# A two-layer decoder trunk on one core: norm inputs scaled ahead on GpSimd, squares added there, waits tile by tile, and an output projection in K halves

## The reference

```python
for l in range(DEPTH):                       # 2 layers
    mod = (c_act @ p['w_ada'][l] + p['b_ada'][l])[:, None, :]
    sh1, sc1, g1, sh2, sc2, g2 = split_cols(mod, [D_MODEL] * 6)
    h = rms_norm(x, p['norm_mix'][l]) * (1.0 + sc1) + sh1
    y = even_mixer(h, ...) if l % 2 == 0 else odd_mixer(h, ...)   # in-projection, recurrence and
                                             # pooling / convolution, out-projection @ w_out
    x = x + g1 * y
    h = rms_norm(x, p['norm_mlp'][l]) * (1.0 + sc2) + sh2
    x = x + g2 * sq_relu_mlp(h, p['mlp_w_up'][l], p['mlp_w_down'][l])
y = rms_norm(x, p['norm_final'])
```

## Time and profile before

| what | value |
|---|---|
| median of three runs | 2791.52 us (2789.2 to 2792.09) |
| the profiled execution | 2792.04 us, of it span 2789.5 us |
| TensorE matmul busy | 2628.9 us (94%), mean granted clock 0.967 |
| VectorE busy | 1583.7 us (57%) |
| ScalarE busy | 985.7 us (35%) |
| GpSimd busy | 276.3 us (10%) |
| chain that ended last | TensorE 82%, VectorE 8%, DMA 6% |
| DMA | 616.13 MB, mean 221 GB/s |

### The profile page before, as it was taken

The page is one execution under the profiler, slowest core; times in us unless marked ns, Lnnn a source line. Parts: engine busy times, 40 slices in busy tenths (PEclk is TensorE's granted clock), DMA queues, the critical chain, the costliest instruction groups (busy, mean ns, idle before and its releaser), DMA issues.

```text
span 2789.5 us, 54649 instructions
## 1 busy us (share of the span) xinstructions
PE 2628.9 (94%) x22440; PEld 2457.6 (88%) x22440; DVE 1583.7 (57%) x2332; ACT 985.7 (35%) x1079; POOL 276.3 (10%) x250
## 2 busy tenths in 40 slices
PE   6799989989999999999997999988899999999998
PEld 3389878979999999999996998988899999999998
DVE  2346354465445545545545998984565565565653
ACT  1133324333223322332333444444343333333333
POOL 1102050010000000000002334530100000000000
PEclk9599999999999999999998999998999999999999
DMA  9977887869999999999753454453455555555553
GB/s 327 336 247 227 281 249 250 276 216 299 301 300 297 297 297 297 297 298 297 236 166 120 151 159 155 136 178 100 144 168 181 181 181 181 181 181 183 181 176 106
DMA packets 589978, 616.13 MB, mean 221 GB/s; under 512 B 10431, under 2 KB 584093, under 8 KB 589313
## 3 DMA queue, kind: packets, MB, share of 16 engines
q1 hardware_dynamic: 583154, 591.70, 67.4%
q0 software_dynamic: 6720, 22.96, 2.6%
HBM read 602.77 MB, written 13.26 MB: 221 GB/s over the span
## 4 chain that ended last, share of the span: by engine, by line
PE 82%; DVE 8%; DMA 6%; issue 1%; ACT 1%; POOL 1%; SPq 0%; DVEq 0%; ACTq 0%; POOLq 0%
PE ps L743 24%; PE ps L744 23%; PE ps L745 23%; PE pm L806 5%; DMA araw_first<-in_w_ada 3%; DVE h_lo L1774 2%; DMA out_new_gla_sample<-st 1%; DVE z L2073 1%; PE pm L821 1%; PE pm L908 1%; DVE w_lo L1650 1%; DMA out_new_hgrn_sample<-st 1%; PE pm L759 1%; DVE acc L2073 1%; PE ps L806 1%
## 5 line engine op out<-in xcount | busy, mean ns | idle before, releaser
L1650 DVE TENSOR_TENSOR w_lo<-raw,w_hi 128x1024 fp32r<-128x1024 f32 x705 | 873.2, 1240 | 983.8 <-ACT w_hi L1244 983.1
L1244 ACT ACTIVATE w_hi<-raw 128x1024 fp32r<-128x1024 f32 x736 | 778.9, 1060 | 1564.5 <-PE ps L745 1503.5
L743 PE MATMUL ps<-h_hi,w_hi 128*128 128x264 f32 x3840 | 1124.7, 293 | 47.6 <-DVE conv_w L2048 16.6
L745 PE MATMUL ps<-h_hi,w_lo 128*128 128x264 f32 x3840 | 1100.6, 287 | 0.0
L744 PE MATMUL ps<-h_lo,w_hi 128*128 128x264 f32 x3840 | 1099.9, 286 | 0.0
L743 PEld LDWEIGHTS ps<-h_hi,w_hi 128*128 128x128 f32 x3840 | 735.8, 192 | 81.6 <-issue 51.4
L744 PEld LDWEIGHTS ps<-h_lo,w_hi 128*128 128x128 f32 x3840 | 736.5, 192 | 0.7
L745 PEld LDWEIGHTS ps<-h_hi,w_lo 128*128 128x128 f32 x3840 | 732.8, 191 | 0.0
L743 PE MATMUL ps<-f_hi,w_hi 128*128 128x264 f32 x2048 | 588.2, 287 | 0.0
L745 PE MATMUL ps<-f_hi,w_lo 128*128 128x264 f32 x2048 | 581.0, 284 | 0.0
L744 PE MATMUL ps<-f_lo,w_hi 128*128 128x264 f32 x2048 | 580.1, 283 | 0.0
(11 more groups left out here) (294 smaller groups left out, 1459.1 us busy)
## 6 DMA issues: line engine op xcount, KB each, us to landing
araw<-in_w_ada SPq DMA_DIRECT2D x160, 1024.0 KB, 8.7
raw<-in_mlp_w_up SPq DMA_DIRECT2D x128, 1024.0 KB, 5.5
raw<-in_mlp_w_down SPq DMA_DIRECT2D x128, 1024.0 KB, 5.4
raw<-in_od_w_in SPq DMA_DIRECT2D x48, 1024.0 KB, 5.3
araw_first<-in_w_ada SPq DMA_DIRECT2D x32, 1024.0 KB, 10.1
raw<-in_ev_w_in SPq DMA_DIRECT2D x32, 1024.0 KB, 5.9
raw<-in_ev_w_out SPq DMA_DIRECT2D x16, 1024.0 KB, 5.6
raw<-in_od_w_out SPq DMA_DIRECT2D x16, 1024.0 KB, 5.4
```

Source lines behind the costliest of these rows:

```text
L743: nc.tensor.matmul(acc, w_hi[:, u, cols], xh[:, k, :], start=(k == 0), stop=False)
L745: last = nc.tensor.matmul(acc, w_lo[:, p, u, cols], xh[:, k, :], start=False, stop=(k == KT - 1))
L1244: nc.scalar.activation(w_hi[:, u, :], raw[:, p, u, :], ACT.Copy).then_inc(hi_ready, 1)
L1650: nc.vector.tensor_tensor(w_lo[:, p, u, :], raw[:, p, u, :], w_hi[:, u, :].bitcast(F32), ALU.subtract).then_inc(lo_ready, 1)
```

## The change

Five things are changed; the initial norm (r = 0) keeps its way.

1. GpSimd gets `norm_work`. While x is made, for each group it multiplies the new pair of x by amod into a new tile `xa` and adds the pair's squares to a new tile `sqa`. TensorE sums only sqa (between units 2 and 3 of the last group) and the last pair.
2. `gains` is moved to before the phase that makes x. For that the order in which the modulation's columns are made is changed in the first layer: SC2 in in0, SH2 in out0.
3. In the last group of out0, of the first MLP and of out1 (`ends`), VectorE evacuates before the last low weights of the next group.
4. `modulate_tiles` takes the place of `modulate`: VectorE scales xa in batches of 1, 1, 2, 4, 4 and 4 tiles and makes the low parts; GpSimd has no part in it. In units 0 and 1 TensorE waits for each tile; the loop over K tiles is now the outer one in a unit and that over the two banks the inner one. conv_w is made before the last chunk of the first MLP.
5. The first two groups of out1 are done together: first the units 0 and 1 of both, then the units 2 and 3 of both, with the LayerNorm's sums between the first four. `raw` and `w_lo` hold one K half of both.

```diff
+            def norm_work(r):
+                pool.wait_ge(ss_done, 7 + r)
+                nc.gpsimd.memset(sqa[:, :, :], 0.0).then_inc(sq_added, 1)
+                if r < 4:
+                    pool.wait_ge(amod_ready, r + 1)
+                for i in range(KT // 2):
+                    k = 2 * i
+                    if r < 4:
+                        pool.wait_ge(x_ready, X_BASE[r] + i + 2)
+                        nc.gpsimd.tensor_tensor(xa[:, k:k + 2, 0:TP], x[:, k:k + 2, 0:TP],
+                                                amod[:, k:k + 2, 0:1].broadcast_to([P, 2, TP]), ALU.mult)
+                        nc.gpsimd.tensor_tensor(xa[:, k:k + 2, TP:T], x[:, k:k + 2, TP:T], amod[:, k:k + 2, 1:NC],
+                                                ALU.mult).then_inc(xa_ready, 1)
+                    if i < KT // 2 - 1:
+                        pool.wait_ge(sq_ready, 8 * r + i + 1)
+                        pool.wait_ge(sq_added, 8 * (r - 1) + 2 + i)
+                        nc.gpsimd.tensor_tensor(sqa[:, :, :], sqa[:, :, :], sq[:, i % 2, :, :], ALU.add).then_inc(sq_added, 1)
...
+            def unit(slot, u, w, p, xh, xl, ready):
+                for kk in range(UK):
+                    ready(u, kk)
+                    k = UK * u + kk
                     for m in range(MT):
                         acc = ps[:, MT * p + m, 0:T]
...
+                def earlier_squares():
+                    pe.wait_ge(sq_added, 8 * norm + 1)
+                    sums(sqa[:, :, :], True)
...
-                for p in range(2):
-                    one(p, p)
-                clear_sums()
-                sums(norm, 0, 0)
-                with pe.Fori(0, count // 2 - 1) as j:
-                    for p in range(2):
-                        i = 2 * j + (2 + p)
-                        one(i, p)
-                        sums(norm, i - 1, 1 - p)
-                sums(norm, count - 1, 1)
+                one(count - 2, 0)
+                one(count - 1, 1, earlier_squares)
+                pe.wait_ge(sq_ready, 8 * norm + 8)
+                sums(sq[:, 1, :, :], False).then_inc(ss_done, 1)
...
             def h_wait(n):
-                return lambda u: pe.wait_ge(h_ready, KT * n + UK * (u + 1))
+                def ready(u, kk):
+                    if u < 2:
+                        pe.wait_ge(h_ready, KT * n + UK * u + kk + 1)
+                    elif kk == 0:
+                        pe.wait_ge(h_ready, KT * n + UK * (u + 1))
+                return ready
...
+            g = G0["out1"]
+            for v in range(2):
+                for u in range(NU):
+                    i = u // 2
+                    if v == 0 and u % 2 == 0:
+                        pe.wait_ge(evacuated, g - 1 + i)
+                    low_ready(g + v, u)
+                    unit(u, 2 * v + u % 2, v, i, h_hi, h_lo, mix_wait(1))
+                    if v == 0 and u == 1:
...
+                        ln_sums(3, (6, 7), 40).then_inc(ln_psum, 1)
+                    if v == 0 and u == 3:
...
+                            last = ln_sums(0, range(4 * j, 4 * j + 4), 32)
+                        last.then_inc(ln_psum, 1)
+            gemm(8, g, h_hi, h_lo, mix_wait(1), norm=3, begun=2)
...
             act.preload_act_table_set("natural_log_exp_and_others")
             g4 = G0["out1"]
-            hi_phase(8, g4, after=square(24, 40), last_next=g4 + 8)
+            split(g4 + 1, 1)
+            split(g4 + 2, 0)
+            for i in range(2):
+                square(3)(i, i)
+            hi_phase(8, g4, after=square(3), last_next=g4 + 8, begun=2)
...
+                    for u in range(NU):
+                        if first and u == NU - 1:
+                            evac(i, p, n + i)
+                        if nxt is not None:
+                            lo(nxt, u, 1 - p)
...
+            def modulate_tiles(r, l, sh):
+                def scale(b):
+                    k0, n = BATCHES[b]
+                    nc.vector.tensor_tensor(xa[:, k0:k0 + n, 0:TP], xa[:, k0:k0 + n, 0:TP],
+                                            rstd[:, 0:TP].unsqueeze(1).broadcast_to([P, n, TP]), ALU.mult).then_inc(hs_done, 1)
+                def low(k):
+                    dve.wait_ge(hh_ready, KT * r + k + 1)
+                    nc.vector.scalar_tensor_tensor(h_lo[:, k, 0:TP], xa[:, k, 0:TP], mod[:, l, sh + k, 0:1],
+                                                   h_hi[:, k, 0:TP].bitcast(F32), ALU.add, ALU.subtract).then_inc(h_ready, 1)
+                dve.wait_ge(rstd_ready, r + 1)
+                dve.wait_ge(xa_ready, KT // 2 * r)
...
+                scale(0)
+                scale(1)
...
+                low(0)
+                scale(2)
+                low(1)
+                scale(3)
+                low(2)
+                low(3)
+                scale(4)
+                for k in range(4, 8):
+                    low(k)
+                scale(5)
+                for k in range(8, KT):
+                    low(k)
...
+            def layer1_first():
+                dve.wait_ge(mod_ready, ADA_MLP0 + 24)
+                gains(2, 1, VA["norm_mix"] + KT, SC1)
+                dve.wait_ge(cw_psum, 1)
+                nc.vector.tensor_copy(conv_w[:, :, :],
+                                      pm[:, 2, 0:8 * TAPS].rearrange("p (j r) -> p j r", r=TAPS)).then_inc(conv_step, 1)
```

More of the change, by code:

```diff
@@ L190, in build @@
         hs = at("hs", [P, 4, TP], F32, o_sq)
+        sqa = sb("sqa", [P, MT, T])
         o_mw = arena(8192)
@@ L519, in _ @@
                 group(N1 + i, i % 2, w, c * GC, 0)
-            phase(8, G0["out1"], kview(io["od_w_out"][0]), lambda i: i * GC)
+            w, g = kview(io["od_w_out"][0]), G0["out1"]
+            for v in range(2):
+                for h in range(2):
+                    sp.wait_ge(split_used, NU * (g + v - 2) + (2 * h + 2))
+                    sp.dma_start(raw[:, v, 2 * h:2 * h + 2, :].rearrange("p u (k n) -> p (u k) n", n=GC),
+                                 w[:, 8 * v:8 * v + 8, h * GC:(h + 1) * GC]).then_inc(raw_in[v][h], 16)
+            phase(6, g + 2, w, lambda i: (i + 2) * GC)
             mlp_layer(1)
@@ L735, in products @@
                 for u in range(NU):
-                    ready(u)
                     low_ready(g, u)
+                    unit(u, u, p, p, xh, xl, ready)
+                    if between:
+                        between(u)
+            def unit(slot, u, w, p, xh, xl, ready):
+                for kk in range(UK):
+                    ready(u, kk)
+                    k = UK * u + kk
                     for m in range(MT):
                         acc = ps[:, MT * p + m, 0:T]
-                        for kk in range(UK):
-                            k = UK * u + kk
-                            cols = slice(kk * GC + m * P, kk * GC + (m + 1) * P)
-                            nc.tensor.matmul(acc, w_hi[:, u, cols], xh[:, k, :], start=(k == 0), stop=False)
-                            nc.tensor.matmul(acc, w_hi[:, u, cols], xl[:, k, :], start=False, stop=False)
-                            last = nc.tensor.matmul(acc, w_lo[:, p, u, cols], xh[:, k, :], start=False, stop=(k == KT - 1))
@@ L746, in products @@
-                    last.then_inc(split_used, 1)
-                    if between:
-                        between(u)
-            def clear_sums():
-                nc.tensor.matmul(pm[:, 0, 0:T], ones[:, :], zero[:, :].broadcast_to([P, T]), start=True, stop=False,
-                                 skip_group_check=True)
-            def sums(norm, i, parity):
-                pe.wait_ge(sq_ready, norm + i + 1)
-                for m in range(MT):
-                    last = nc.tensor.matmul(pm[:, 0, 0:T], ones[:, :], sq[:, parity, m, :], start=False,
-                                            stop=False, skip_group_check=True)
-                last.then_inc(ss_done, 1)
@@ L763, in gemm @@
-            def gemm(count, g, xh, xl, ready, norm=None, a0=None):
-                def one(i, p):
-                    if a0 is None:
-                        products(g + i, p, xh, xl, ready)
-                        return
-                    ada_group(a0 + i, "pm")
-                    products(g + i, p, xh, xl, ready, lambda u: ada_turn(a0 + i, "pm") if u == 1 else None)
+                        cols = slice(kk * GC + m * P, kk * GC + (m + 1) * P)
+                        nc.tensor.matmul(acc, w_hi[:, slot, cols], xh[:, k, :], start=(k == 0), stop=False)
@@ new lines, in unit, with sums @@
+                        nc.tensor.matmul(acc, w_hi[:, slot, cols], xl[:, k, :], start=False, stop=False)
+                        last = nc.tensor.matmul(acc, w_lo[:, w, slot, cols], xh[:, k, :], start=False, stop=(k == KT - 1))
+                last.then_inc(split_used, 1)
+            def sums(src, first):
+                for m in range(MT):
+                    last = nc.tensor.matmul(pm[:, 0, 0:T], ones[:, :], src[:, m, :], start=(first and m == 0),
```

(28 more changed lines are left out.)

207 lines of the change are left out of this document (104 added, 103 removed).

## The result

The changed kernel takes 2757.36 us (median of four runs, 2752.86 to 2759.76); the kernel before took 2790.36 us beside it (four runs, 2788.67 to 2792.09). The ratio is 0.988, with a 95% interval of 0.9863 to 0.9897: faster by 33 us, where 50.6 were forecast. The profiled execution has 2752.86 us and a span of 2751.0 us, with a mean granted clock of 0.972. It is the fastest of the four, so the profiles differ by 39.2 us and the medians by 33.0.

A forecast was written before the change was run, and what follows sets the result against it. The prediction took TensorE to bound the kernel. Its terms, 19.8 + 17.7 - 0.8 + 6.1 + 7.5 + 0.3 = 50.6 us, came off the profiled 2792.04 us, giving 2741.4, median 2741 us; range 2732 to 2756.

The forecast's parts named there:

- Step 5: Order inside a unit: more bank changes and waits in groups fed by h, taken as 0, bounds 0 to 13 us.
- Step 1: Four norms: adding squares on GpSimd takes 4.95 us off TensorE in each, 19.8 us in all.
- Step 2: Last evacuation ahead of the last low weights: the square starts 2.2 us earlier in S1, S2 and S3.
- S2: Seam after the first MLP: glu starts without waiting behind conv_w, gain 17.7 us; conv weights' transposes cost 0.8 elsewhere.
- Step 3: Modulation after rstd, tile by tile without GpSimd: gains 17.7 us in S2, 6.1 in S3, 7.5 in S1.
- S3: Seam after out1: the first group's last two units end earlier, gain 6.1 us.
- S1: Seam after out0: gated by mod_rows after unit 1, gain 7.5 us, 2.3 more if the clock does not fall.
- Step 4: Opening of out1 with K halves first: wait moves from h_lo to w_lo, gain 0.3 us, bounds -3 to +5.4.
- (a): Rival: GpSimd or the gates eat part of the seams, about 4 us x 3, 2753 us; chance 0.15.
- (b): Rival: kinder clock in S1 and S2's sums, K halves worth 5.4 us, 2733 us; chance 0.12.
- (c): Rival: waits inside units 0 and 1 of groups fed by h break TensorE's stream, 125 us, 2866; chance 0.05.
- (d): Rival: in S2 a wait holds TensorE's first product until all h_lo are there, 2751 us; chance 0.06.

The follow-up runs named there:

- the experiment: Changed kernel with squares summed pair by pair on TensorE again, GpSimd only multiplying x by amod: 2776.62 us.
- the early split: Changed kernel with the weights of out1's second K halves split during the variance, ahead of the LayerNorm's end: 2751.18 us.
- its experiment: Changed kernel with TensorE waiting for h once a unit instead of for single tiles, order of banks kept: 2759.22 us.
- the last experiment: Changed kernel with banks outer except glu's first group, sqa allocated last, second K halves split early, rates' rows copied after the fifth low tile: 2733.24 us.

## Why the prediction was right and wrong

The sign was right, the size wrong: 2757.36 us lies 1.4 us above the range, and the gain is 33.0 us instead of 50.6. Of the 17.6 us of gain that are missing, 11.4 are in the profiled executions, which differ by 39.2. The other 6.2 are where these stand: after's is 4.5 below its median, before's 1.7 above. A forecast made against one execution carries that error whatever its steps.

**Step 5 failed**, the order inside a unit, taken as 0. The runs show 0.16 us a group in its place, 10.2 us over the second MLP's 64 groups, where the forecast misses 10.0. Its reasoning saw two things that could cost, the bank's change and the waits, and both cost nothing. It didn't see the third, that the order of the loops is also the order in which operands are read, nor that a new tile ahead of the others shifts their addresses. The bound of 13 us was too small: the order alone costs 26.4 us on the kernel before (19.7 in the profiles). The sign that was to show step 5 wrong, a pitch longer by more than 0.003 us, was too coarse as well: 0.1208 became 0.1224, 0.0016 more, and over 17664 products that is 28 us. Taken out of the kernel after, the order gives 8.9 us back, and with the addresses on top the forecast of the second MLP's segment is met.

**Step 1 was right, but for out0.** Its four terms of 4.95 measured 3.0, 5.2, 5.4 and 4.5. The small one is out0's, the term that was mis-sized, though 1.45 of its shortfall lie in out0's first group, which has no sums (17.51 us in the experiment, 18.96 in after). Among the six groups behind the first, one takes 14.91 us with its sums (the experiment) and 14.20 without (after, median): 0.71 and not 0.90. Without them TensorE comes to wait for the modulation, 0.23 and 0.36 us in two of these groups, a gate that step 1 left out when it called out0 a stretch of busy products:

```profile
479.26 1.50 PE L846 MATMUL pm<-araw,c_pad 128*32 128x256 f32 x24 [0.23 <-DVE mod L1757]
```

The starts of the groups divide up the 5.35 us that are missing up to R1. Ahead of out0 1.4 us are lost: in0's sixteen groups take 319.0 us instead of 315.8 (320.2 with the order alone on the kernel before), and they start 1.8 earlier. out0's first group takes 18.96 us instead of 16.82; kernels that do the same there have 17.5 or 19.0, for which no cause was looked for. The six groups behind it gain 4.1 us and not 5.85, and the stretch behind them 1.15 for 1.3. Of the 1.7 that the six groups lack, 1.2 are the sums (89.9 us with them and 85.3 without) and 0.5 the order (89.4 before). The order has a share in in0's 3.2 as well, whose size stays open.

**Step 2 was right.** At S2 3.3 us lay between the last product's end and the square, and 1.1 do now.

**Step 3 was right, seam by seam.** From the last product before the seam on, S2 gives 18.6 us for 17.7 (the surplus is the 1.0 of the sums at full clock), S3 6.3 for 6.1, S1 8.5 for 7.5; the 0.8 for the conv weights lies elsewhere. The gates are those named: h_lo for the first product, mod_rows after unit 1 in S1 (2.56 us). The delay by which the subtraction might hold up GpSimd came and fitted, 1.06 us for 1.2: in each of the three seams GpSimd's last product takes 2.10 us instead of 1.04, beside a subtraction of 1.23, and in S2 it is done at 1463.67, when rstd only starts. The Trainium skill (SBUF — State Buffer, "SBUF: two separate sides") says that whichever of the two comes first has the port for its whole instruction. By that rule the product would end at 1461.54 + 1.23 + 1.04 = 1463.81, and the trace agrees within 0.14 us. It goes the other way round too: in out1 a subtraction that starts inside a product of GpSimd takes 1.48 us, and GpSimd's next operation, of only 16 elements, takes 1.20:

```profile
1893.33 1.05 POOL L602 TENSOR_TENSOR xa<-x,amod 128x512 f32<-128x512 f32 x1 [46.13 <-DVE x L1803]
1894.34 1.20 POOL L604 TENSOR_TENSOR xa<-x,amod 128x16 f32<-128x16 f32 x1
1893.98 1.48 DVE L1712 TENSOR_TENSOR w_lo<-raw,w_hi 128x1024 fp32r<-128x1024 f32 x1 [0.79 <-ACT w_hi L1296]
```

**Step 4 was right**: w_lo is the releaser of the second halves, the variance runs at full clock (3.72 for 3.6), and out1 opens no earlier in substance. Its upper bound of 5.4, if the weights come by then, was a sound price for an edit: the early split opened the second halves 5.4 us earlier and gave 6.2 in the medians (4.0 from LN to R3 in the profiles).

**The rivals.** (a) didn't come: VectorE's low tiles follow at 0.40 (3.25 us for eight). Of (b)'s three parts one came, the sums of S2 at full clock (1.0 us); S1 fell to half clock after its wait, and the K halves gave nothing. (c) fell with its experiment. (d) was not what happened, and its price of 10 us measured 6.7 in the medians and 9.4 in the profiles' segment from R2 to LN. That the time came near (a)'s and (d)'s is chance; no cause that they name is in the trace.

**Open.** The order costs 26.4 us on the kernel before, and its removal from the kernel after gives 8.9. Part of the difference is that both effects don't add: order alone has a pitch of 11.76, addresses alone 11.67, and both together 11.76 again. Another part is what the old order costs at the seams, where four tiles must be there at once. What is left wasn't traced to a cause. Nor was the mechanism: that TensorE's products follow each other more slowly in one order and from some addresses is shown, and why isn't. The loss isn't in one place: the mean distance behind the first, second and third product of a K tile in the second MLP is 121.2, 120.2 and 121.1 ns before, and 122.3, 122.4 and 122.8 after. The segment from R2 to LN gained 2.8 us more than forecast. Its opening, up to the transpose inside glu, gives 15.4 us for 15.5, so the surplus lies behind it, in the mixer. It is within what kernels differ by that do the same there (406.8 to 409.5 us in four of after's kind, 419.7 to 425.9 in five of before's), for which no cause was looked for.

## What to carry to other kernels

When TensorE bounds a phase and is busy all the time, compare the number of matmuls in windows of equal length: 1.3% fewer was most of the error here, and no busy share, clock or wait showed it. An edit that reorders a hot loop has a second effect besides its waits and its banks, the order of operand reads, and an edit that allocates a tile has one on every tile behind it; both are priced by one run each, with nothing else changed. In the last experiment, where the new tile is allocated last, the pitch is that of before.

## What the runs showed of the hardware that was not expected

- A group of 96 products of 264 columns takes 11.60, 11.67 or 11.76 us at the same clock, by the order in which its operands are read and the low part of the inputs' addresses. 64 bytes more in front cost 4.4 us over 64 groups; 2048 bytes cost nothing.
- A change of the accumulating bank after 3 products instead of 12 costs nothing (2485 products in 300 us), and so do waits that are already satisfied (11.76 us a group with and without them).
- GpSimd's product of 512 elements takes 1.04 us alone and 2.10 when it starts 0.03 us behind a VectorE subtraction, which itself keeps its 1.23 us. A subtraction that starts while GpSimd's product runs takes 1.48.
